# Dividing softmax rows: the prompt attention's probability rows move from GpSimd and VectorE to ScalarE

## The reference, cut to what matters

```python
s = (jnp.einsum('bqhr,bkr->bhqk', qlb, c_kv)
     + jnp.einsum('bqhp,bkp->bhqk', qrb, k_r)).astype(jnp.float32)
s = jnp.where(kpos[None, :] <= qpos[:, None], s, -jnp.inf)
p = jax.nn.softmax(s, axis=-1).astype(c_kv.dtype)
return jnp.einsum('bhqk,bkr->bqhr', p, c_kv)
```

## Time and profile before

| | |
|---|---|
| median of three runs | 1322.11 us |
| the profiled execution's own time | 1322.68 us |
| its span in the trace | 1321.0 us |
| TensorE busy over the span | 1282.6 us (97%) |
| VectorE busy | 834.7 us (63%) |
| ScalarE busy | 514.8 us (39%) |
| GpSimd busy | 424.7 us (32%) |
| divides on GpSimd (L922) | 48, 49.6 us |
| divides on VectorE (L2383) | 16, first at 228.1 us, last at 419.8 us |
| exponentials on ScalarE (L1803) | 64, first at 222.8 us, last at 418.4 us |

### The profile page before, as it was taken

How to read it: one execution, slowest core, us unless ns; L and a number is a source line. 1 busy time by engine, 2 the same in 40 slices (tenths; PEclk the granted TensorE clock), 3 DMA queues, 4 the chain that set the end, 5 groups by cost and what they waited for, 6 DMA issues and landing times.

```text
span 1321.0 us, 23688 instructions
## 1 busy us (share of the span) xinstructions
PE 1282.6 (97%) x9274; PEld 1202.8 (91%) x9274; DVE 834.7 (63%) x1258; ACT 514.8 (39%) x902; POOL 424.7 (32%) x279
## 2 busy tenths in 40 slices
PE   8999999999999999999999999999999999999997
PEld 7788998888787569999999999999999999999987
DVE  5884166777775436178945455354644479899977
ACT  6323235666665333025322232222222234544462
POOL 2633344453432126741243434344434300000000
PEclk8999998999998999999999999999999999999999
DMA  9311102000027535530222122212222289757503
GB/s 325 134 62 33 33 20 74 5 21 1 17 68 263 174 150 200 190 103 21 98 74 85 62 81 88 74 65 81 81 74 90 71 328 344 252 179 259 172 1 135
DMA packets 70376, 151.56 MB, mean 115 GB/s; under 512 B 9138, under 2 KB 16690, under 8 KB 69842
## 3 DMA queue, kind: packets, MB, share of 16 engines
q1 hardware_dynamic: 70290, 150.39, 33.6%
HBM read 127.80 MB, written 22.56 MB: 114 GB/s over the span
## 4 chain that ended last, share of the span: by engine, by line
PE 83%; DVE 8%; issue 3%; ACT 2%; DMA 2%; POOL 1%; SPq 0%; DVEq 0%; POOLq 0%; ACTq 0%
PE ps L1013 25%; PE ps L1014 24%; PE ps L1015 24%; PE ps L1242 2%; DMA araw<-in_w_dn 2%; PE ps L1300 1%; PE ps L1362 1%; PE ps L1254 1%; PE ps L1255 1%; DVE nmx L2389 1%; ACT pTH L1635 1%; PE ps L1021 1%; PE ps L1327 1%; DVE pTL L2406 1%; DVE prob L2383 0%
## 5 line engine op out<-in xcount | busy, mean ns | idle before, releaser
L982 POOL TENSOR_TENSOR ws<-wraw,ws 128x1024 fp32r<-128x1024 f32 x50 | 124.5, 2490 | 214.1 <-ACT ws L1635 214.1
L1013 PE MATMUL ps<-bHL,aHL 128*128 128x272 f32 x616 | 178.3, 289 | 4.3 <-DVE bHL L2834 4.1
L1015 PE MATMUL ps<-bHL,aHL 128*128 128x272 f32 x616 | 177.2, 288 | 0.0
L1014 PE MATMUL ps<-bHL,aHL 128*128 128x272 f32 x616 | 177.1, 288 | 0.0
L2677 DVE TENSOR_TENSOR bufP<-bufP,ps 128x544 f32<-128x544 f32 x66 | 47.5, 721 | 134.3 <-PE ps L1015 132.0
L1635 ACT ACTIVATE ws<-wraw 128x1024 fp32r<-128x1024 f32 x55 | 58.4, 1062 | 172.6 <-PE ps L1015 168.7
L1013 PEld LDWEIGHTS ps<-bHL,aHL 128*128 128x128 f32 x616 | 116.0, 188 | 5.6 <-DVE bHL L2834 5.6
L1014 PEld LDWEIGHTS ps<-bHL,aHL 128*128 128x128 f32 x616 | 116.0, 188 | 0.0
L1015 PEld LDWEIGHTS ps<-bHL,aHL 128*128 128x128 f32 x616 | 115.9, 188 | 0.0
L1005 POOL TENSOR_TENSOR rt<-ms,mhalf 128x3 f32<-128x3 f32 (+1 forms) x3 | 4.4, 1463 | 250.5 <-DVE ms L2868 250.5
L1635 ACT ACTIVATE aHL<-araw 128x512 fp32r<-128x512 f32 x66 | 41.7, 632 | 97.5 <-PE ps L1015 58.3
(11 more groups left out here) (378 smaller groups left out, 4463.6 us busy)
## 6 DMA issues: line engine op xcount, KB each, us to landing
araw<-in_w_dn SPq DMA_DIRECT2D x121, 256.0 KB, 3.5
wraw<-in_w_gu SPq DMA_DIRECT2D x44, 512.0 KB, 3.5
cp<-in_cache SPq DMA_DIRECT2D x64, 272.0 KB, 4.8
ab<-acts SPq DMA_DIRECT2D x34, 272.0 KB, 5.1
raw<-in_w_out SPq DMA_DIRECT2D x16, 512.0 KB, 4.5
acts<-bufC SPq DMA_DIRECT2D x22, 272.0 KB, 2.1
xt<-in_x_tok SPq DMA_DIRECT2D x9, 512.0 KB, 5.7
x<-x2s SPq DMA_DIRECT2D x8, 544.0 KB, 6.4
```

The costliest lines, as they stand in the source:

```text
L982: pool.tensor_tensor(w[:, 1, :], w_source(j), w[:, 0, :], ALU.subtract).then_inc(cw_lo, 1)
L1013: nc.tensor.matmul(out, wh, xh, start=start, stop=False)
L1014: nc.tensor.matmul(out, wh, xl, start=False, stop=False)
L1015: return nc.tensor.matmul(out, wl, xh, start=False, stop=stop)
```

## The change

All 64 divides are done by ScalarE, as a copy with a scale that is read from `rsm`, one number for each partition (`hi(row, row, rsm)`). The divide of row qi - 1 stands behind the exponential of row qi. The divide of row 3 stands behind the divide of row 2 where the next step of `move_turned` would not come or is the unit's end, and behind the next `pTH` where there is one (second unit of a pair). GpSimd's `normalise` and VectorE's divide in `invert` are gone. Semaphores and who waits for them stay as they were.

```diff
-            def normalise(u):
-                for qi in range(3):
-                    r, qt = 4 * u + qi, 4 * (u % 2) + qi
-                    n = P * (qt + 1)
-                    row = prob[:, prob_at(qt):prob_at(qt) + n]
-                    pool.wait_ge(s_rc, r + 1)
-                    pool.tensor_tensor(row, row, rsm[:, r % 4:r % 4 + 1].broadcast_to((P, n)),
-                                       ALU.mult).then_inc(s_pn, 1)
...
-            normalise(0)
...
-                if u < UNITS - 1:
-                    normalise(u + 1)
...
+            def divide(u, qi):
+                r, qt = 4 * u + qi, 4 * (u % 2) + qi
+                row = prob[:, prob_at(qt):prob_at(qt + 1)]
+                act.wait_ge(s_rc, r + 1)
+                hi(row, row, rsm[:, r % 4:r % 4 + 1]).then_inc(s_pn if qi < 3 else s_pd, 1)
...
                         exponential(u + 1, qi)
+                        if qi:
+                            divide(u + 1, qi - 1)
+                    if kt and row_at(u, kt - 1) == 3:
+                        divide(u + 1, 3)
...
+                if u + 1 < UNITS and row_at(u, 4 * blk + 3) == 3:
+                    divide(u + 1, 3)
...
             for qi in range(4):
                 exponential(0, qi)
+                if qi:
+                    divide(0, qi - 1)
+            divide(0, 3)
...
                 nc.vector.reciprocal(rsm[:, s], sm[:, s]).then_inc(s_rc, 1)
-                if qi == 3:
-                    qt = 4 * (u % 2) + 3
-                    row = prob[:, prob_at(qt):prob_at(qt + 1)]
-                    dve.wait_ge(s_rc, r + 1)
-                    nc.vector.tensor_scalar(row, row, rsm[:, s], None, ALU.mult).then_inc(s_pd, 1)
```

## The result

The changed kernel took 1346.0 us (median of four runs, 1344.29 to 1350.85), the kernel before 1322.73 us in the same comparison. The ratio is 1.0175 (95% interval 1.0158 to 1.0193), so about 23 us more. The forecast was 1348.5. The text calls the stretch from a unit's last products to the first turns of the next a seam, `pTH` the high-part move and `pTL` the low-part move.

A forecast was written before the change was run, and what follows sets the result against it. The prediction took a ring of waits through ScalarE, VectorE and TensorE at unit ends as the bound. Terms 20.6 + 4.4 + 0.3 + 0.5 = 25.8 us on 1322.68 gave 1348.5 us, 8-in-10 range 1335 to 1361.

The forecast's parts named there:

- Which engine bounds the stage: At unit ends, a ring of waits through ScalarE, VectorE and TensorE sets the time, despite ScalarE's 80 us free.
- The price of a divide: On ScalarE, 0.39 us for 128 columns up to 1.14 for 1024; 48.9 us for all divides.
- Even units: Eight units, 2.78 us each: 1.64 ahead of the maximum, 1.14 behind the exponential; less 0.5 and 1.14, 20.6 us.
- signs of being wrong: Even units growing under 2 us, granted clock falling behind a pair's first unit, or later stages changing length.
- Second units: Second unit of each pair, four: divides ahead of the last high-part moves cost 1.1 us each, 4.4 us in all.
- Fourth units: Three with a successor: divides fit ScalarE's 1.80 us wait for queries and keys; 0.1 each, 0.3 us.
- Start: Unit 0's first turn waits for all four divides; 1.2 us where reciprocal and VectorE's divide took 0.7: +0.5 us.
- The clock: Rival: TensorE's clock falls at four seams behind first units of pairs, +12.4 us, 1361 us; chance 0.12.
- Nothing else changes: Behind the stage, everything starts later by the same amount; no later wait keeps its old time.
- Not slower: Rival: TensorE bounds the seams and ScalarE's room holds the divides; -3.9 us, about 1319 us; chance 0.03.
- only the ends count: Rival: the 640, 768 and 256 divides fall into ScalarE's waits; 11.4 us remain, 1334 us; chance 0.17.
- ScalarE as the bound: Rival: ScalarE bounds the whole stage, so 48.9 us less VectorE's 13.6 count: +35.3, 1358 us; chance 0.13.

The follow-up runs named there:

- inline: Kernel before with only the 640- and 768-column divides on ScalarE, ahead of the even unit's last high-part move: 1340.79 us, ratio 1.0127.
- inwait: Kernel before with the same 16 divides on ScalarE, behind the even unit's last high-part move, ahead of the 1024-column exponential: 1324.32 us, ratio 0.9999.
- rows23: Kernel before with only the divides of rows 2 and 3 on ScalarE, placed as in the change; rows 0 and 1 on GpSimd: 1333.92 us, ratio 1.0070.
- late: Changed kernel with all 64 divides still on ScalarE, but those outside fourth units placed in ScalarE's waits: 1330.08 us, ratio 1.0042 to the kernel before.
- warm: Changed kernel plus eight 512-column matmuls nobody reads at each seam behind a pair's first unit: 1347.4 us, ratio 1.0185 to the kernel before.
- warm_again: Changed kernel with the same eight added matmuls per seam, repeated on one chip beside the changed kernel: 1349.57 us, ratio 1.0184 to the kernel before.

## Why the prediction was right, point by point

*Which engine bounds the stage:* right. The ring through ScalarE, VectorE and TensorE ended the units, and ScalarE's free time didn't count. Shown by inline against inwait.

*The price of a divide:* right, 49.1 us in all for 48.9 forecast. What I took off for the start ahead of the predecessor's end, 0.05, was too little: the divide behind an accumulator read starts 0.1 us ahead of its end (290.62, 293.35, 297.04), and the move behind a divide as well (294.17, where the divide ends at 294.28). For the same reason ScalarE was busy 173 us in the stage, not the 184 forecast: 49.1 us of durations added only 38.5 to the 134.96 of the earlier trace rows.

*Even units:* right in kind, too large in size. 2.78 forecast, 2.28 to 2.33 measured in five of the distances (the sixth, 2.92, has a low clock in it). Ahead of the maximum it was 1.33 instead of 1.64, behind the exponential 1.01 instead of 1.14. Unit 0's share hidden in its wait was 0.6 (1.72 left), and the last even unit kept about 1.4 of 1.64. Forecast 20.6, measured 1.72 + 6 x 2.33 + 1.4 = 17.1.

By the measure that the prediction named, first `pTH` to first `pTH`, the first units of a pair grew by 1.96 us where the clock stayed (10.06 to 12.02), the third units by 2.31 and unit 0 by 1.35; the second units grew by 1.36. What a first unit lacks stands in the second: there `hv` comes behind the turn, and its delay of 0.37 falls into the next unit. The two measures give the same total. But two of the prediction's own signs of being wrong have thereby come up: even units under 2 us, and a clock that fell behind first units. They don't touch the ring itself, whose cost was sized 24% too large (25.8 for 20.8 in all); they do show that the clock had no term.

*Second units:* 1.1 forecast, 0.98 in the table where the clock stayed (12.37 less 11.39). Of that 0.58 for 384 and 512 (rows23), the other 0.40 for 256. Forecast 4.4, measured 3.9.

*Fourth units:* 0.3 in all forecast, none measured (9.40 for 9.42; first `pTH` to first `pTH` 22.06 to 22.12 for 22.09 to 22.14). VectorE's two divides of 2.33 us, whose going was counted as hidden there, gave nothing back either. *Start:* + 0.5 forecast, - 0.15 measured (7.07 for 7.22); over all kernels this distance varied from 6.68 to 7.23, with the clock low there in each, so the term isn't resolved.

*The clock:* this was a rival with a chance of 0.12 and 12.4 us, and the sum held nothing for it. It happened twice in the first profile and three times in the second, though only three of the five falls were in the seams that the rival named. Each cost 1.0 to 2.5 us, the next distance included, instead of 3.1. Why they cost less than that isn't shown; that TensorE waits for part of a unit anyway is a guess. In the first profile the falls are 2.5 us of the 21.9, and the ring gives the other 19.5, or 20.8 with the last even unit. The runs agree: their median clock was 0.9865 in the first comparison and 0.984 in the last, where before had 0.990, so by 0.6 to 0.9 us for each 0.001 the clock is worth an estimated 2 to 5 us of the 23 or 24. So the hit on 23 is partly luck, two errors of opposite sign: terms too large by 5.0 us (25.8 for 20.8), and no term for the clock.

*Nothing else changes:* nearly. From the sample tokens' first exponential to the end of the span it took 879.0 us for 878.9. The stage began 1.72 us earlier in the profile after (221.06 against 222.78) though nothing ahead of it was touched; over the kernels run here it began between 221.06 and 223.84. Profiles differ by this much before the change has begun.

*The other rivals:* all three fell. Not slower, because the turn moved; only the ends count, because 640 and 768 inline cost 1.33 in an even unit; ScalarE as the bound, because all 64 divides cost 6 us in other places (late).

## What to carry to other kernels

An engine that is idle for a third of a stage isn't free: find for each place in its order which instruction behind it is waited for. The same 16 instructions cost 16 us ahead of a move that others wait for (about 10 of delay, the rest with a lower clock) and nothing directly behind it; so an added piece of work goes behind the last thing that others need, into the wait for a long producer. And where a delayed instruction feeds two strands, relieving one of them gives back only part: 0.5 to 0.8 us a unit of the 1.4 expected.

## What the hardware showed that was not expected

TensorE's clock fell from 2.4 to 1.2 GHz (granted 0.50) behind short waits: in the seam behind a first unit after one of 1.34 us, and at the end of a second unit after three of 0.65, 0.22 and 0.84 us within 4 us. It did so at 2 or 3 of the stage's 8 such places, and at others in the next execution of the same kernel. The profile of warm has the waits of 0.64, 0.22 and 0.84 us too, and the clock stayed at 1.00 there, where warm_again fell twice. So equal work and equal waits don't mean an equal clock.

The clock goes with the time of the single run. In the last comparison the changed kernel's five runs go from 1346.72 us at 0.989 to 1352.62 us at 0.982, and the 15 of before from 1320.73 at 0.992 to 1326.62 at 0.989. A difference of a few us between two kernels says little until their granted clocks have been set side by side.
